# Two-block transformer kernel: attention outputs of the mixer written turned, and probabilities scaled before their transposes

## The reference

```
p = e / denom                      # softmax of the masked scores
o_a = swa(...)                     # window of 128, with sinks in the denominator
o_b = g0 * o_cmp + g1 * o_sel + g2 * o_win     # per token and head
o_c = mla(...)
merged = g[0] * (o_a @ w_br_a) + g[1] * (o_b @ w_br_b) + g[2] * (o_c @ w_br_c)
x = x + merged @ w_out
```

## Time and profile before

| | us |
|---|---|
| three runs | 1772.38, 1773.39, 1773.91 (median 1773.39) |
| profiled execution, its own time | 1768.87 |
| its span, first to last instruction | 1766.8 |
| TensorE busy in it | 1653.2 (94%) |
| VectorE busy | 912.0 (52%) |
| ScalarE busy | 640.0 (36%) |
| mean granted TensorE clock | 0.973 of full |

### The profile page before, as it was taken

One profiled execution on the slowest core, in us unless ns is written; L12 is line 12 of the kernel. 1 busy time (PEld: TensorE's weight loads), 2 busy tenths in 40 slices (PEclk: granted clock), 3 DMA queues, 4 the chain that ended last, 5 costly groups with the idle time before them and its releaser, 6 DMA issues.

```text
span 1766.8 us, 22391 instructions
## 1 busy us (share of the span) xinstructions
PE 1653.2 (94%) x9411; PEld 1268.4 (72%) x9411; DVE 912.0 (52%) x1295; ACT 640.0 (36%) x928; POOL 27.4 (2%) x89
## 2 busy tenths in 40 slices
PE   5999999989999979989999799999989999989998
PEld 1997556444434447777878699988758788779986
DVE  2686446352111135466575566645636658555653
ACT  1443212010000024355644534444345564444432
POOL 1000001010000000000000000000000000000000
PEclk9899889979999989999999999999999999999999
DMA  8455255377999964414245345555331334525552
GB/s 296 162 191 187 101 188 194 143 292 277 408 410 410 410 243 150 156 50 145 93 167 191 97 150 185 191 191 187 143 119 50 142 136 175 185 98 182 182 185 88
DMA packets 165246, 333.27 MB, mean 189 GB/s; under 512 B 17571, under 2 KB 69029, under 8 KB 165157
## 3 DMA queue, kind: packets, MB, share of 16 engines
q1 hardware_dynamic: 159312, 325.89, 50.7%
q10 hardware_dynamic: 5846, 6.11, 1.0%
HBM read 330.94 MB, written 1.05 MB: 188 GB/s over the span
## 4 chain that ended last, share of the span: by engine, by line
PE 76%; DVE 9%; DMA 8%; ACT 4%; issue 2%; POOL 0%; SPq 0%; POOLq 0%; DVEq 0%; ACTq 0%
PE ps_g L693 19%; PE ps_g L674 16%; DMA arena<-in_w_up_dram 6%; PE ps_g L1175 5%; PE ps_g L1058 4%; PE ps_s L1369 3%; PE ps_p L1369 3%; PE ps_g L838 3%; PE ps_o L748 3%; DVE ring_r L2026 2%; PE ps_s L719 1%; PE ps_s L674 1%; PE ps_p L674 1%; PE ps_x L647 1%; PE ps_p L738 1%
## 5 line engine op out<-in xcount | busy, mean ns | idle before, releaser
L2026 DVE TENSOR_TENSOR ring_r<-ring,late_w 128x4096 fp32r<-128x4096 f32 (+1 forms) x50 | 217.0, 4339 | 148.7 <-ACT late_w L1616 148.7
L1616 ACT ACTIVATE late_w<-ring 128x4096 fp32r<-128x4096 f32 (+1 forms) x50 | 178.1, 3562 | 126.8 <-PE ps_p L1369 42.8
L693 PE MATMUL ps_g<-h_t_r,late_w 128*128 128x256 f32 x640 | 179.3, 280 | 0.0
L693 PE MATMUL ps_g<-hf_high,ring_r 128*128 128x256 f32 x640 | 179.0, 280 | 0.0
L693 PE MATMUL ps_g<-hf_high,late_w 128*128 128x256 f32 x576 | 162.1, 281 | 0.0
L1058 PE MATMUL ps_g<-ring,arena 128*64 128x512 f32 x384 | 112.1, 593 | 10.6 <-DMA arena<-in_w_up_dram 9.1
L693 PEld LDWEIGHTS ps_g<-hf_high,ring_r 128*128 128x128 f32 x640 | 122.0, 191 | 0.0
L693 PEld LDWEIGHTS ps_g<-h_t_r,late_w 128*128 128x128 f32 x640 | 120.7, 189 | 0.0
L693 PEld LDWEIGHTS ps_g<-hf_high,late_w 128*128 128x128 f32 x576 | 108.1, 188 | 0.0
L1058 PEld LDWEIGHTS ps_g<-ring,arena 128*64 128x64 f32 x384 | 35.8, 137 | 81.8 <-issue 81.8
L1640 ACT ACTIVATE arena<-arena,neg_max 128x256 f32<-128x256 f32 (+1 forms) x160 | 71.5, 449 | 60.5 <-DVE neg_max L2078 60.5
(11 more groups left out here) (656 smaller groups left out, 3745.4 us busy)
## 6 DMA issues: line engine op xcount, KB each, us to landing
ring<-in_w_in_dram SPq DMA_DIRECT2D x31, 2048.0 KB, 7.6
ring<-in_w_gate_up_dram SPq DMA_DIRECT2D x44, 1024.0 KB, 6.9
ring<-in_w_gate_dram SPq DMA_DIRECT2D x16, 2048.0 KB, 16.9
arena<-in_w_down_dram SPq DMA_DIRECT2D x16, 2048.0 KB, 14.8
ring<-in_w_mod_dram SPq DMA_DIRECT2D x12, 2048.0 KB, 12.6
ring<-in_w_down_dram SPq DMA_DIRECT2D x10, 2048.0 KB, 7.7
ring<-in_w_up_dram SPq DMA_DIRECT2D x8, 2048.0 KB, 18.1
arena<-in_w_up_dram SPq DMA_DIRECT2D x8, 2048.0 KB, 23.0
```

The lines of the kernel that those rows point to most:

```text
L693: ins = pe.matmul(b.ap[:, (f % 2) * SEQ:(f % 2 + 1) * SEQ], a[:, k, f * P:(f + 1) * P], x[:, k, :], start=k == 0 and i == 0, stop=k == nk ...
L1616: act.activation(high_of(name, rnd)[:, 0:n], ring[:, slot, 0:n], ACT.Copy).then_inc(high_ready.sem, 1)
L2026: dve.tensor_tensor(ring_r[:, slot, 0:n], ring[:, slot, 0:n], high_of(name, rnd)[:, 0:n].bitcast(F32), ALU.subtract).then_inc(low_ready.se ...
```

## The change

VectorE no longer divides the outputs. A new part norm(n) (mixer_norm) takes one over the sum, times the branch gate, and multiplies the probabilities of step n in the buffer scores with it, in place, before they are transposed; turn(n) now waits for norm(n) instead of exp(n). In VectorE's program norm(0) stands behind mask(1), and in round n the order is norm(n+1), mask(n+2), take(n), make_gate_low. The waits and the work after steps 0, 2, 3, 4 and 15 keep their places.

output(n) has its operands exchanged: v (64 columns) is stationary and probs_t moves (128 columns). Heads 0 and 2 of the step go to partitions 0 to 63 of bank O and heads 1 and 3 to partitions 64 to 127, one after the other in turn, and the result has channels on the partitions. A "cmp" step has four products of 128 columns instead of one of 512.

take(n) (mixer_take) copies or adds bank O into o_turned. The transposes behind the loop, their copies and subtractions go. Instead split_high and split_low make the high and low part of each o in one operation of 128x1024, from SBUF: high of "a" on ScalarE after make_high("bra"), of "b" in step 16, of "c" after the last step; low of "a" on VectorE ahead of take(17), behind a wait for the last gate product, "b" and "c" after it. TensorE waits for o_low_ready ahead of bra, brb and brc. The places of oa_high and oa_low in SBUF are exchanged, and the cross attention's o_x has the place of o_a. Nothing changes in the loads of weights or in the other parts of the kernel.

```diff
-LAYER_USES = {"G0": 33, "G1": 33, "S": 30, "P": 30, "O": 45, "X": 30}
+LAYER_USES = {"G0": 33, "G1": 33, "S": 30, "P": 30, "O": 42, "X": 27}
...
-        cmp_tmp = arena[:, at + 3136:at + 3136 + HALF].rearrange("p (h d) -> p h d", d=HD)
-        o_a, o_b, o_c = (view(at + 1024 * i, TB, HALF) for i in range(3))
+        o_turned = {name: view(at + 1024 * i, KF, SEQ) for i, name in enumerate("abc")}
+        o_x = view(at, TB, HALF)
...
-        o_low = {"a": view_r("oa_low", LAT_AT - 1024, KF, SEQ), "b": view_r("ob_low", SLOT, KF, SEQ), "c": view_r("oc_low", ROT_AT, KF, SEQ)}
-        o_high = {"a": view_r("oa_high", ROT_AT + 1024, KF, SEQ), "b": view_r("ob_high", KT_AT, KF, SEQ), "c": view_r("oc_high", KT_AT + 1024, KF, SEQ)}
+        o_low = {"a": view_r("oa_low", ROT_AT + 1024, KF, SEQ), "b": view_r("ob_low", SLOT, KF, SEQ), "c": view_r("oc_low", ROT_AT, KF, SEQ)}
+        o_high = {"a": view_r("oa_high", LAT_AT - 1024, KF, SEQ), "b": view_r("ob_high", KT_AT, KF, SEQ), "c": view_r("oc_high", KT_AT + 1024, KF, SEQ)}
...
+        normed_p = Named(sem("probs_normed"), layer=(LAYERS, [step_tag(s) for s in MIXER_STEPS]))
+        o_high_ready, o_low_ready = sem("o_high_ready"), sem("o_low_ready")
...
-            def turn_probs(part, step, rnd=0):
+            def turn_probs(part, step, rnd=0, ready=probs):
...
-                pe.wait_ge(probs.sem, probs.at(part, tag, rnd))
+                pe.wait_ge(ready.sem, ready.at(part, tag, rnd))
...
-                        turn_probs("layer", step, l)
+                        turn_probs("layer", step, l, normed_p)
...
                 def mixer_output(n):
 
                     step = MIXER_STEPS[n]
-                    if step[0] == "cmp":
-                        claim(O, step_tag(step), l)
-                        pe.wait_ge(PT.free, PT.nth("layer", step_tag(step), l))
-                        pe.matmul(O.ap[:, :], probs_t[:, 0, 0, :], cmp_v[:, :, :].rearrange("p h d -> p (h d)"), start=True, stop=True)\
-                            .then_inc(O.full, 1)
-                    elif step[0] == "mla":
-                        output_step("layer", step, lambda s, i, b: mla_v[:, b, (4 * s[1] + i) * HD:(4 * s[1] + i + 1) * HD], l)
-                    else:
-                        at_v = {"swa": C_AV, "sel": C_VS, "win": C_VW}[step[0]]
-                        output_step("layer", step, lambda s, i, b: proj[:, b, at_v + HD * (i // 2):at_v + HD * (i // 2 + 1)], l)
+                    kind, pp, _ = step
+                    claim(O, step_tag(step), l)
+                    pe.wait_ge(PT.free, PT.nth("layer", step_tag(step), l))
+                    if kind == "cmp":
+                        for m in range(KF):
+                            ins = pe.matmul(O.ap[:, m * P:(m + 1) * P], cmp_v[:, 2 * m:2 * m + 2, :].rearrange("p h d -> p (h d)"), probs_t[:, 0, 0, :],
+                                            start=True, stop=True)
+                        ins.then_inc(O.full, 1)
+                        return
+                    kbs = keys_of(step) // P
+                    for m in range(2):
+                        for b in range(kbs):
+                            for r in range(2):
+                                i = 2 * m + r
+                                if kind == "mla":
+                                    v = mla_v[:, b, (4 * pp + i) * HD:(4 * pp + i + 1) * HD]
+                                else:
+                                    at_v = {"swa": C_AV, "sel": C_VS, "win": C_VW}[kind]
+                                    v = proj[:, b, at_v + HD * m:at_v + HD * (m + 1)]
+                                ins = pe.matmul(O.ap[r * HD:(r + 1) * HD, m * P:(m + 1) * P], v, probs_t[:, i, b, :], start=b == 0, stop=b == kbs - 1)
+                    ins.then_inc(O.full, 1)
...
-                for name, src in (("a", o_a), ("b", o_b), ("c", o_c)):
-                    if name == "b":
-                        pe.wait_ge(rows.sem, rows.at("layer", "ob", l))
-                    else:
-                        pe.wait_ge(O.free, O.nth("layer", step_tag((SWA_STEPS if name == "a" else MLA_STEPS)[-1]), l))
-                    turn_rows(f"o{name}", [lambda tb, k=k, s=src: s[:, tb, k * P:(k + 1) * P] for k in range(KF)], l)
...
-                for name in "ab":
-                    turned("layer", f"o{name}", 2, l)
+                for j, name in enumerate("ab"):
+                    pe.wait_ge(o_low_ready, 3 * l + j + 1)
...
-                turned("layer", "oc", 2, l)
+                pe.wait_ge(o_low_ready, 3 * l + 3)
...
+                def split_high(name, after):
+
+                    act.wait_ge(O.free, O.nth("layer", step_tag(after), l))
+                    act.activation(o_high[name][:, :, :], o_turned[name][:, :, :], ACT.Copy).then_inc(o_high_ready, 1)
...
                         make_high("bra", l)
+                        split_high("a", SWA_STEPS[-1])
+                    if n + 2 == len(MIXER_STEPS):
+                        act.wait_ge(S.full, S.nth("layer", step_tag(MIXER_STEPS[-1]), l))
+                        split_high("b", WIN_STEPS[-1])
...
-                for name in "abc":
-                    turned_high(f"o{name}", KF, o_high[name], l)
+                split_high("c", MLA_STEPS[-1])
...
-                def mixer_finish(n):
+                def mixer_norm(n):
 
                     step = MIXER_STEPS[n]
-                    if step[0] == "swa":
-                        finish_step("layer", step, crossed(o_a)(step), l)
-                    elif step[0] == "sel":
-                        finish_step("layer", step, crossed(o_b)(step), l, branch(1, step), first=True)
-                    elif step[0] == "cmp":
-                        finish_blocks(n, step)
-                    elif step[0] == "win":
-                        ins = finish_step("layer", step, crossed(o_b)(step), l, branch(2, step))
-                        if step == WIN_STEPS[-1]:
-                            ins.then_inc(rows.sem, 1)
-                        else:
-                            st.done(ins)
-                            st.settle()
+                    kind, tag = step[0], step_tag(step)
+                    if kind == "cmp":
+                        total_blocks(n, step)
+                        dve.tensor_tensor(block_scores(n), block_scores(n), over(rden[:, n % 2, :], CMP), ALU.mult).then_inc(normed_p.sem, 1)
+                        return
+                    total, inv = den[:, n % 4, 0:4], rden[:, n % 2, 0:4]
+                    dve.wait_ge(probs.sem, probs.at("layer", tag, l))
+                    if kind == "swa":
+                        st.done(dve.tensor_tensor(total, total, sink_e[:, n % 4, 4:8], ALU.add))
+                        st.settle()
+                    st.done(dve.reciprocal(inv, total))
+                    st.settle()
+                    if kind in ("sel", "win"):
+                        inv4 = inv.rearrange("p (f r) -> p f r", f=2)
+                        st.done(dve.tensor_tensor(inv4, inv4, branch(1 if kind == "sel" else 2, step), ALU.mult))
+                        st.settle()
+                    s = scores[:, n % 2, 0:4, 0:keys_of(step)]
+                    dve.tensor_tensor(s, s, over(inv, keys_of(step)), ALU.mult).then_inc(normed_p.sem, 1)
+
+                def mixer_take(n):
+
+                    kind, pp, qb = step = MIXER_STEPS[n]
+                    tokens = slice(qb * P, (qb + 1) * P)
+                    dst = o_turned["c" if kind == "mla" else "a" if kind == "swa" else "b"]
+                    if kind == "mla":
+                        dst = dst[:, 2 * pp:2 * pp + 2, tokens]
+                    elif kind == "cmp":
+                        dst = dst[:, :, tokens]
                     else:
-                        finish_step("layer", step, o_c[:, step[2], step[1] * SEQ:(step[1] + 1) * SEQ].rearrange("p (i d) -> p i d", d=HD), l)
+                        dst = dst.rearrange("p (f a) n -> p f a n", a=2)[:, :, pp, tokens]
+                    dve.wait_ge(O.full, O.nth("layer", step_tag(step), l))
+                    src = O.ap[:, 0:dst.shape[1] * P].rearrange("p (m n) -> p m n", n=P)
+                    if kind in ("cmp", "win"):
+                        dve.tensor_tensor(dst, src, dst, ALU.add).then_inc(O.free, 1)
+                    else:
+                        dve.tensor_copy(dst, src).then_inc(O.free, 1)
+
+                def split_low(name):
+
+                    j = "abc".index(name)
+                    dve.wait_ge(o_high_ready, 3 * l + j + 1)
+                    dve.tensor_tensor(o_low[name][:, :, :], o_turned[name][:, :, :], o_high[name][:, :, :].bitcast(F32), ALU.subtract).then_inc(o_low_ready, 1)
...
                 mixer_mask(1)
+                mixer_norm(0)
                 for n, step in enumerate(MIXER_STEPS):
-                    if step[0] == "cmp":
-                        total_blocks(n, step)
+                    if n + 1 < len(MIXER_STEPS):
+                        mixer_norm(n + 1)
```

(9 more changed lines are left out.)

17 lines of the change are left out of this document (5 added, 12 removed).

## The result

The changed kernel takes 1776.34 us (median of 20 runs, 1771.29 to 1779.55); the kernel before, run beside it, 1772.2 us (20 runs, 1767.54 to 1776.41). The ratio is 1.002, with a 95% interval of 1.001 to 1.0029: some 4 us slower, at the edge of what can be told from no change. The forecast was 1776.6 us, +3.2. The profiled execution took 1776.33 us, with a span of 1774.3.

A forecast was written before the change was run, and what follows sets the result against it. TensorE, busy 94% of the span, was taken as the bound. A to E sum to -2.0 us a layer and F adds +3.6: +3.2 us in all, 1776.6 us against the median of 1773.39; range 1767 to 1785.

The forecast's parts named there:

- A: Loop start: turn(0) waits for norm(0) behind mask(1), 2.8 us later, and VectorE's chain to mask(3) lengthens; +3.8 us a layer.
- B: Output steps: paired lane halves make 16 records take 0.96 us instead of 1.73, less two shape changes; -5.8 us a layer.
- C: ScalarE: high copies of a and b in steps 14 and 16 delay later exponentials and copies; +1.1 us a layer.
- D: Loop end: turn(17) waits for norm(17) behind the 128x4096 subtraction on VectorE; +3.9 us a layer.
- E: Behind the loop: transposes, high copies and low subtractions between output(17) and bra go; -5.0 us a layer.
- F: Granted clock falls at the new waits at turn(0) and turn(17); +3.6 us a layer, bounds 0 and 5.8.
- The drain: Rival at output steps: each change of the array's shape costs a whole drain; 1781 us, chance 0.13.
- The rival that it holds: Rival: the granted clock holds in all waits, so nothing is lost to it; 1769.4 us, chance 0.25.
- halves do not run side by side: Rival at output steps: lane halves do not overlap, or only partly; 1787.6 us with the clock lost too, chance 0.15.

The follow-up runs named there:

- e3: Changed kernel with the high copy of a moved on ScalarE from step 14 to step 16, ahead of that of b; 1775.6 us.
- e1: Changed kernel with the 128x4096 subtraction for bra moved on VectorE from behind take(15) to behind take(16); 1766.2 us.
- e13: Changed kernel with 28 transposes of the identity filling TensorE's wait at turn(17) alone; 1774.0 us.
- e12: Changed kernel with the later subtraction for bra and later high copy of a, plus 28 identity transposes filling the wait at turn(0); 1765.4 us.
- e4: Changed kernel with the products of V and probabilities issued one lane half after the other instead of alternating; 1779.1 us.

## Why the prediction was right, by its steps

The sum per term, for both layers: -4.0 for A to E, and +7.2 for F. By the stretches above the loops became 3.8 us shorter apart from the clock behind the two new waits, and 6.4 us went to that. That makes +2.7 in the loops (with rounding), against +3.2. The terms as measured one by one, below, come to -2.0 a layer.

- **A, +3.8 a layer.** turn(0) waited 4.00 us for 4.1 forecast. Against the kernel before the waits grew by 2.76 us at turn(0), 1.12 at turn(2) and 0.18 at scores(4), and one of 0.23 at output(0) went: 3.8.
- **B, -5.8.** The size came out, by two errors that cancel, and that is luck. 16 records take 1.02 us and 8 records 0.59 us to the next instruction; forecast were 1.16 and 0.68. With 1.73 and 0.84 before, that alone would be -7.7 (8 x 0.71 and 8 x 0.25). But the neighbours grew: the last gate product is followed after 0.32 us instead of 0.23, and the first transpose behind the output after 0.165 us instead of 0.115. Over 16 steps that takes back 16 x 0.14 = 2.2 us and leaves -5.5. Not the loading of 64 columns at 60 ns sets the pace, as assumed, but the streaming of 128 at 107 ns a pair. And an output takes half its records x 107 ns plus 0.16 us, so the two changes of shape cost 0.16 + 0.09 + 0.05 = 0.30 us, where 0.2 was taken.
- **The drain**, by the Trainium skill, TensorEngine Tiling (Array Packing), section Key Properties: it says that changing the tiling mode drains the array. The trace agrees that a change costs time: 0.15 us each, which is nearer to the 0.17 of the rival's whole drain than to the 0.1 of the forecast. So that rival had the price nearly right; its 1781 us did not come, since the pairs ran at 107 ns instead of 120.
- **C, +1.1.** 0.74 + 0.57 = 1.31 us of waits, for 1.4 forecast, and small waits changed by -0.4 for -0.3 forecast: +0.9. e3 takes back 1.9 us in both layers.
- **D, +3.9.** 3.80 us; e1 removes it, and turn(16) to bra becomes 4.3 us shorter a layer: 3.0 of it waits (3.80 + 0.29 became 0.25 + 0.89) and 1.3 clock.
- **E, -5.0.** 7.03 us from output(17) to bra became 1.38: 5.65 less, of which 0.64 are B's (1.73 became 1.09 there), so -5.0. bra waited 0.29 us, 0.3 forecast. b and c ended under bra.
- **F, +3.6 a layer.** The clock fell behind all four waits. At turn(0) that cost 1.5 us in layer 0, where the low stretch was 3.4 us long, and 2.3 in layer 1, where it was 6.8; at turn(17) it cost 1.3 in each. So F was +2.8 and +3.6, for 2.35 + 1.2 forecast. The rival that it holds falls for waits of this length. But the term took the clock as a matter of the waits alone. e13 bears that out at turn(17); e12 shows that at turn(0) filling the wait can be followed by a fall elsewhere that costs as much.
- **The rival "halves do not run side by side"** falls by the 64 ns a record of the changed kernel, and e4 shows where pairing ends.

The absolute figure came out within 0.3 us; that is partly luck, since before and changed kernel each scatter by 8 to 9 us.
